# New start addresses, modulo 256 bytes, for the tiles that TensorE reads beside the weight tiles

## What is computed

```python
def first_block(x, mem, ...):
    mem_n = rmsnorm(mem, mem_norm)
    h = x
    for l in range(2):
        hn = rmsnorm(h, mix_norm[l])
        h = h + (short_conv_pool_mixer(hn, ...) if l % 2 == 0 else sparse_attn_hgrn_mixer(hn, ...))
        h = h + memory_cross_attn(rmsnorm(h, xattn_norm[l]), mem_n, ...)
        h = h + peer_ffn(rmsnorm(h, peer_norm[l]), ...)
    return rmsnorm(h, final_norm)

def peer_ffn(h, wq, sub_keys, u, v):
    ...
    act = gelu(einsum('td,ted->te', xb, u[eid]))
    return einsum('te,ted->td', g * act, v[eid])

def second_block(x, ...):
    for layer in range(2):
        hn = _rmsnorm(h, attn_norm[layer])
        h = h + (_even_mixer(hn, ...) if layer % 2 == 0 else _odd_mixer(hn, ...))
        h = h + _swiglu(_rmsnorm(h, ffn_norm[layer]), w_gate_up[layer], w_down[layer])
    return _rmsnorm(h, final_norm)
```

## Time and profile before

| | before |
|---|---|
| median of three runs | 2813.01 us |
| the profiled execution's own time | 2813.5 us |
| its span, first to last instruction | 2811.2 us |
| TensorE, VectorE, ScalarE busy | 97%, 73%, 52% |
| mean granted TensorE clock | 0.99 |
| read from HBM | 505.53 MB |

### The profile page before, as it was taken

How to read it: one execution, slowest core, us unless ns; L and a number is a source line. 1 busy time by engine, 2 the same in 40 slices (tenths; PEclk the granted TensorE clock), 3 DMA queues, 4 the chain that set the end, 5 groups by cost and what they waited for, 6 DMA issues and landing times.

```text
span 2811.2 us, 57248 instructions
## 1 busy us (share of the span) xinstructions
PE 2714.5 (97%) x19552; PEld 2544.1 (90%) x19552; DVE 2053.1 (73%) x4430; ACT 1454.5 (52%) x2378; POOL 177.8 (6%) x141
## 2 busy tenths in 40 slices
PE   7999999999999999989999999999999989999998
PEld 6999899999988888979998999988888889999998
DVE  8557997886566667876699888567776877666665
ACT  5455345444555555555544444455555565446544
POOL 0004000000000000000374000000000100000000
PEclk9999999999999999999999999999999999999999
DMA  5445566455766665424456555676666525563454
GB/s 190 176 157 184 204 215 213 174 182 195 261 242 242 242 242 179 149 78 165 165 182 217 191 172 183 218 258 242 242 242 242 187 81 182 190 230 117 177 184 178
DMA packets 140451, 546.19 MB, mean 194 GB/s; under 512 B 15784, under 2 KB 81592, under 8 KB 83616
## 3 DMA queue, kind: packets, MB, share of 16 engines
q1 hardware_dynamic: 63216, 455.38, 44.8%
q10 hardware_dynamic: 73728, 67.14, 7.4%
q0 software_dynamic: 3376, 21.88, 2.0%
HBM read 505.53 MB, written 40.91 MB: 194 GB/s over the span
## 4 chain that ended last, share of the span: by engine, by line
PE 78%; DVE 15%; DMA 2%; ACT 2%; issue 2%; DVEq 0%; ACTq 0%; SPq 0%
PE bank L796 23%; PE bank L797 23%; PE bank L798 23%; PE bank L1016 4%; DVE wL L551 4%; DMA ring<-in_w_stream 2%; PE bank L917 1%; ACT wH L540 1%; PE bank L937 1%; DVE pr_eq L1969 1%; DVE pr_eq L1971 1%; DVE pr_m L1973 1%; PE bank L928 1%; DVE pr_m L1924 0%; DVE pr_i L1924 0%
## 5 line engine op out<-in xcount | busy, mean ns | idle before, releaser
L551 DVE TENSOR_TENSOR wL<-ring,wH 128x1024 fp32r<-128x1024 f32 x809 | 988.1, 1224 | 605.5 <-ACT wH L540 602.5
L540 ACT ACTIVATE wH<-ring 128x1024 fp32r<-128x1024 f32 x864 | 907.3, 1055 | 423.2 <-DMA ring<-in_w_stream 252.6
L796 PE MATMUL bank<-hnH,wH 128*128 128x256 f32 x3528 | 1003.3, 284 | 34.5 <-DVE wL L551 26.6
L797 PE MATMUL bank<-hnL,wH 128*128 128x256 f32 x3528 | 984.0, 279 | 0.0
L798 PE MATMUL bank<-hnH,wL 128*128 128x256 f32 x3528 | 983.5, 279 | 0.0
L796 PEld LDWEIGHTS bank<-hnH,wH 128*128 128x128 f32 x3528 | 667.5, 189 | 45.7 <-issue 22.9
L797 PEld LDWEIGHTS bank<-hnL,wH 128*128 128x128 f32 x3528 | 667.2, 189 | 0.5 <-issue 0.2
L798 PEld LDWEIGHTS bank<-hnH,wL 128*128 128x128 f32 x3528 | 665.1, 189 | 0.0
L796 PE MATMUL bank<-wH,wgtH 128*128 128x512 f32 x1024 | 398.5, 389 | 0.3 <-DVE wgtL L2010 0.3
L798 PE MATMUL bank<-wH,wgtL 128*128 128x512 f32 x1024 | 398.4, 389 | 0.0
L797 PE MATMUL bank<-wL,wgtH 128*128 128x512 f32 x1024 | 398.3, 389 | 0.0
(11 more groups left out here) (411 smaller groups left out, 3535.3 us busy)
## 6 DMA issues: line engine op xcount, KB each, us to landing
ring<-in_w_stream SPq DMA_DIRECT2D x432, 1024.0 KB, 4.9
act_parked<-act_out ACTq DMA_DIRECT2D x256, 128.0 KB, 3.0
act_in<-act_parked ACTq DMA_DIRECT2D x256, 128.0 KB, 2.7
sw_bias<-in_c_swa POOLq DMA_DIRECT2D x1, 4096.0 KB, 15.7
relb_rows<-rel_table POOLq DMA_DIRECT2D x1, 2048.0 KB, 10.0
h_parked<-h POOLq DMA_DIRECT2D x2, 1024.0 KB, 6.3
h_back<-h_parked POOLq DMA_DIRECT2D x2, 1024.0 KB, 6.2
od_relb<-relb_rows POOLq DMA_DIRECT2D x2, 1024.0 KB, 7.4
```

The source lines that it names most:

```text
L540: eng.activation(wH[:, b % NBUF, :], raw(b), ACT.Copy).then_inc(w_high, 1)
L551: eng.tensor_tensor(wL[:, b % NBUF, :], raw(b), wH[:, b % NBUF, :].bitcast(F32), ALU.subtract).then_inc(w_low, 1)
L796: pe.matmul(dst, lh, rh, start=start, stop=False, skip_group_check=True)
L797: pe.matmul(dst, lh, rl, start=False, stop=False, skip_group_check=True)
```

## The change

Only the places of tiles change. After it, counted from the same point (the weight tiles' address modulo 256):

| tiles | before | after |
|---|---|---|
| `wgtH`, `wgtL` (gated activations), `sq`, `onehot`, `act_in` | 0 | 64 |
| `hnH`, `hnL` (normed rows) | 192 | 128 |
| `att_OTH`, `att_OTL` (attention outputs) | 192 | 128 |
| `ycat`, `pool` halves | 192 | 128 |
| `ff_aH`, `ff_aL` (feed-forward halves) | 192 | 64 |
| `od_yH`, `od_yL` | 192 | 64 |
| `od_hH`; `od_hL` | 192; 192 | 64; 192 |
| `con` | 224 | 128 |
| `memH`, `memL`, `pr_h`, `ml_n`; `pr_q` | 192; 0 | 192; 0 |

`snk` (64 bytes) now stands ahead of `shared`, and `vec` (544) and `rb` (32) stand where `small` and `snk` did, ahead of `hnH`: 64 + 8,192 + 576 = 8,832 bytes, 128 modulo 256.

```diff
             ("att_before", [ATT0], F32), ("att_L", [DEEP, 258], F32), ("att_P", [DEEP, 258], F32),
-            ("att_PT", [DEEP, 256], F32), ("att_O", [2, 1024], F32), ("att_gap", [32], F32),
+            ("att_PT", [DEEP, 256], F32), ("att_O", [2, 1024], F32), ("att_gap", [16], F32),
             ("att_OTH", [8, 256], F32R), ("att_OTL", [8, 256], F32R))
...
-                ("ev_cnt", [4, 256], F32), ("ycat", [4, 256], F32), ("ev_gap", [40], F32), ("poolH", [4, 256], F32R),
+                ("ev_cnt", [4, 256], F32), ("ycat", [4, 256], F32), ("ev_gap", [24], F32), ("poolH", [4, 256], F32R),
...
-        _, od_hH, od_hL = stage(("od_h_before", [8752], F32), ("od_hH", [DC, T], F32R), ("od_hL", [DC, T], F32R))
-        _, od_rels = stage(("od_rels_before", [12848], F32), ("od_rels", [16, T], F32))
+        _, od_hH, _, od_hL = stage(("od_h_before", [8720], F32), ("od_hH", [DC, T], F32R), ("od_h_gap", [32], F32), ("od_hL", [DC, T], F32R))
+        _, od_rels = stage(("od_rels_before", [12880], F32), ("od_rels", [16, T], F32))
...
-                ("od_gap", [32], F32), ("od_relb", [16, 256], F32), ("od_yH", [8, 256], F32R), ("od_yL", [8, 256], F32R),
+                ("od_relb", [16, 256], F32), ("od_gap", [64], F32), ("od_yH", [8, 256], F32R), ("od_yL", [8, 256], F32R),
...
-            ("ff_gap", [48], F32), ("ff_aH", [FC, 256], F32R), ("ff_aL", [FC, 256], F32R))
+            ("ff_gap", [16], F32), ("ff_aH", [FC, 256], F32R), ("ff_aL", [FC, 256], F32R))
         sb("arena", [P, 32768])
         ring = sb("ring", [P, SLOTS, 2 * BLK])
         wH, wL = sb("wH", [P, NBUF, BLK], F32R), sb("wL", [P, NBUF, BLK], F32R)
+        snk = sb("snk", [P, 16])
...
         sb("shared", [P, DC * T])
-        small = sb("small", [P, 96])
-        snk = sb("snk", [P, 16])
+        vec = sb("vec", [P, NVEC])
+        rb = sb("rb", [32, 8])
 
         hnH, hnL = sb("hnH", [P, DC, T], F32R), sb("hnL", [P, DC, T], F32R)
         act_out = sb("act_out", [P, 2, T])
         root_sb, mem_root = act_out[:, 0, :], act_out[:, 1, :]
-        vec = sb("vec", [P, NVEC])
         con = sb("con", [P, NCST])
         iww = sb("iww", [P, DC, 8])
-        rb = sb("rb", [32, 8])
         slotT = sb("slotT", [P, 3, T])
+        small = sb("small", [P, 96])
```

More of the change, by code:

```diff
@@ L385, in build_stacks @@
         _, pr_hH, pr_hL = stage(("pr_h_before", [8240], F32), ("pr_hH", [DC, T], F32R), ("pr_hL", [DC, T], F32R))
-        _, od_hH, od_hL = stage(("od_h_before", [8752], F32), ("od_hH", [DC, T], F32R), ("od_hL", [DC, T], F32R))
-        _, od_rels = stage(("od_rels_before", [12848], F32), ("od_rels", [16, T], F32))
+        _, od_hH, _, od_hL = stage(("od_h_before", [8720], F32), ("od_hH", [DC, T], F32R), ("od_h_gap", [32], F32), ("od_hL", [DC, T], F32R))
+        _, od_rels = stage(("od_rels_before", [12880], F32), ("od_rels", [16, T], F32))
         pr_tv, pr_px, pr_pa, pr_pb, pr_paf, pr_pbf = [pr_m[:, k] for k in range(6)]
         pr_e, pr_g, pr_i1, pr_i2 = [[pr_m[:, 6 + 2 * k], pr_m[:, 7 + 2 * k]] for k in range(4)]
-        od_q, od_ckv, od_ik, od_iq, od_hq, od_hf, od_hg, od_hi, od_ckvn, od_ckvT, od_iw, od_sel, _, od_relb, \
+        od_q, od_ckv, od_ik, od_iq, od_hq, od_hf, od_hg, od_hi, od_ckvn, od_ckvT, od_iw, od_sel, od_relb, _, \
             od_yH, od_yL, od_neg, od_rel, od_sc, hg_A, hg_f, hg_QL0, hg_QL1, hg_KL0, hg_KL1, hg_dq, hg_dk, \
```

## The result

The changed kernel takes **2857.1 us** (median of four, 2854.9 to 2859.7), the kernel before 2812.4 beside it: a ratio of **1.0156, 95% interval 1.0138 to 1.0174**, 44 us slower. The forecast was 2792 with a range from 2758 to 2838. Both lists of instructions are the same on every engine. The profiled execution took 2856.5 us, its span is 2854.3, its mean granted clock 0.99.

What follows compares the result with a forecast made beforehand. The prediction took TensorE's matmul pace to bound the kernel. It summed -21 us for the 256-column streams, 0 for the gated activations and 0 for `onehot`, on 2813 us, giving 2792, with a range from 2758 to 2838.

Steps and rivals of the forecast that it cites:

- What bounds the kernel: Whole kernel: TensorE, busy 97% of the span, bounds it, so how fast one matmul follows another is what counts.
- Taken: -21 us: `hn`, attention outputs, feed-forward and other moved 256-column streams: new addresses end the slow pace; -21 us, bounds -29 and +29.
- the slow pace: 256-column matmul streams: 117.8 ns for each matmul instead of 113.3, a difference of 4.5 ns.
- Taken: 0: Gated stages, 512 columns: moving the gated activations to 64 changes nothing; ends -33 and +14 us kept.
- The floor: Matmul streams: 226.7 ns for 512 columns and 113.3 for 256 look like paces that no address goes under.
- It has no price of its own: `onehot`, both operands of line 1016, moves with the shared tile: may change how a block starts, nothing priced.
- They hinder each other: Slow 256-column streams: weight read and moving-row read both take longer, 192 against 188 and 281 against 276 ns.
- The address alone doesn't choose; it allows or forbids the slow one: `hn` streams: both paces occur at one address; the address allows or forbids the slow one, given how the reads start.
- The new addresses favour the slow pace: Rival, chance 0.25: `hn` at 128 slow everywhere, gated stage 2.2 ns slower; 36 us at most, 2849, half likelier, 2831.
- No effect of addresses: Rival, chance 0.19: block starts cause the slow pace, new addresses leave the mixture as it is; 2813 us.
- the gated stage gains too: Rival, chance 0.15: the gated stages also speed up, -21 - 33 = -54 us, 2759.
- The cover: Ahead of line 796: part of the gain returns where `wL` is late; TensorE already waits 26.6 us there for `hn`.

Runs made afterwards that it cites:

- the probe: Kernel before plus a measuring stretch: 256- and 512-column matmuls, both operands from one weight tile, at eight relations, three starts each; no kernel time given.
- gated_only: Kernel before with only `snk` moved, so gated activations, `onehot` and `sq` stand at 64, `hn` stays at 192; 2843.2 us, ratio 1.0128.
- normed_only: Kernel before with only the normed rows `hn` moved, from 192 to 128; 2833.1 us, ratio 1.0091.
- arena_only: Kernel before with only arena tiles moved: attention outputs, `ycat`, `pool` to 128, feed-forward halves, `od_y`, `od_hH` to 64; 2822.4 us, ratio 1.0044.

## Why the prediction was wrong

**What bounds the kernel** held: TensorE's pace. The span followed the matmul streams and nothing else, VectorE and ScalarE didn't move, and no wait of TensorE grew by more than 1.1 us (ahead of the gated matmuls' line 796, 0.3 to 1.4).

**"Taken: -21 us"** for `hn`, the attention outputs and the feed-forward halves is the step that failed. Its premise was that a new relation forbids the slow pace and leaves 113.3. The prediction itself noted that "no row shows 128 or 64 for a moving tile at all", and then took the change's direction as an improvement. The probe has 118.7 at 128, never 113.3, and a bistable 64. Of the kernel's `hn` streams, 10,284 matmuls, the mean went from 115.4 to 118.8 ns, +35 us; with the pauses between them counted, their distances add up to 1287.6 us before and 1314.1 after, +26.5.

**"Taken: 0" for the gated activations, bounds -33 and +14.** It is +20.5: 3,072 x 6.67. The floor was right: nothing in any run is under 226.7 for 512 columns or 113.3 for 256. But being on the floor meant that each other address could only be worse, and the upper bound came from rows that hadn't the relation in question. The memory values of the earlier trace rows are settled at 228.9 ns, but "the relation turned the other way" was misread: their stationary halves stand at 192 and the weights at 0, which makes 64, and the probe has 229 there. The moved gated activations stand at 64, which makes 192, and there it has 233.0 to 233.7. The slow pace's 4.5 ns belongs to 256 columns.

**"It has no price of its own"** for `onehot` failed in part: with it at 64 hardly a routing block is fast, 5.9 us in `gated_only`. **The range's lower end**, 2758, is called the full gain of both parts, but is worked out with -21; with the bound of -29 it would be 2751.

**The Trainium skill's rules.** All 256-column streams of halves here take 113.3 ns at best and 512-column ones 226.7; full-precision matmuls as in the earlier trace rows are the ones that show 216 ns a record. The Trainium skill, TensorE: Matmul & The Clock Gate, "Back-to-back issue gap", gives N/2.4 + 2.5 ns, which is 109.2 and 215.8, and calls it the gap of an isolated matmul; with halves no relation, width of the stationary operand or start came near either. The Trainium skill, TensorE: Matmul & The Clock Gate, "Step-by-step: what each phase is for", gives weight loads and moving rows a read port each, by which the change would have been free. The Trainium skill, SBUF — State Buffer, "SBUF: two separate sides", likewise has TensorE waiting for nobody there. The measured 113.3 against 120.0 ns for the same instructions eight bytes apart shows a dependence between the two operands' places that none of these rules has. Where inside the chip it arises, no run tells.

**"They hinder each other"** from 281 against 276 and 192 against 188 ns went too far. In the changed kernel the slow `hn` stream has these groups, 690 to 740 us:

```profile
L797 PE MATMUL bank<-hnL,wH 128*128 128x256 f32 x141 | 39.7, 281 | 0.0
...
L796 PEld LDWEIGHTS bank<-hnH,wH 128*128 128x128 f32 x141 | 26.5, 188 | 0.0
```

The matmul's 281 goes with slowness, the load's 192 doesn't: it is 188 at a pace of 118.9.

**"The address alone doesn't choose; it allows or forbids the slow one"** was half right, and had the sign of the danger wrong. A relation decides which paces can be had at all, and more than two exist (113.3, 117.8, 118.7, 120.0); where both 113.3 and 117.8 can, the start or the last pause decides. Most relations lack the fast one. Even 192, the best, doesn't forbid the slow one.

**The rivals.** "The new addresses favour the slow pace" (0.25) is what happened, by its own point of decision: all of `hn` is slow. Its price was too small on both terms: 36 us at most, for it took 117.8 as the slowest pace (118.9 measured) and 7 us for the gated stage (20.5). "No effect of addresses" (0.19) is refuted by `normed_only` and the probe; "the gated stage gains too" (0.15) by every run.

**The cover.** That faster matmuls would run into waits for `wL` was argued in the prediction; it worked the other way round. The waits of TensorE, before and then after the change (us in total, times, longest):

```profile
PE bank L796 <- DVE wL L551: 43.7, 37, 7.2
```

```profile
PE bank L796 <- DVE wL L551: 29.5, 28, 6.0
```

14.2 us of waiting went, which is the 12.9 by which TensorE's free time fell and a bit more. The down products became 4.9 us shorter at an unchanged pace, and the waits ahead of line 796 of the feed-forward halves tell of 3.3 of it (3.9 in the earlier trace rows, 0.6 after).

## What to carry to other kernels

Before the address of an operand is moved, find the relation, moving less stationary start modulo 256, of each matmul stream and the pace that it has now; if the pace is the lowest that any stream of that width shows, leave it. A price for a relation that no row shows has to be measured, in a stretch of a few hundred matmuls at eight relations, since neighbours of the best place are as bad as any. A stage that a padding or a small tile ahead of it shifts belongs to the change as well: here the version that moved `onehot` and `sq` along with the gated activations lost 16 us more than the one that didn't, and half of it is seen in the traces.

## What was not expected of the hardware

- The good place is 8 bytes sharp: 113.3 ns at 192, 120.0 at 184, 119.6 to 121.8 at 200. It is another one for 512 columns (0) than for 256 (192), and 256, 512 or 768 added to the latter change nothing (nine of nine sets at 113.3).
- At one relation a stream can have two paces, and keeps the one that it has over hundreds of matmuls (61 of 61 stretches in the kernel before). A change of tile or group doesn't end it, a pause can, down to a distance of 132 ns instead of 118; behind a short full-precision matmul two of six starts at 64 were fast, six of six at 192, settled within nine matmuls.
- The lowest distances are 113.3 and 226.7 ns at granted clock 1.00 (2.4 GHz), in the ratio of the columns, so the excess over one column a cycle (106.7 and 213.3) is a sixteenth and not a fixed cost. Narrower stationary operands, whose load lasts 108 ns instead of 188, didn't lower it (227.9 to 232.4).
- Open: why the routing blocks alternate with `onehot` at 0 and don't with it at 64; which pace a pause leaves behind; and what takes the last 5 us of `arena_only` and the last 8 of `gated_only`.
